# Product-key experts: dense sums for half the tokens, indirect fetches for the other half

## The reference, cut to what matters

```python
q = (h @ w_pq).reshape(B, S, PEER_HEADS, 2, PEER_QHALF)             # 8 heads, 2 halves of 128
s = jnp.einsum('bshjd,hjnd->bshjn', q, sub_keys)                     # 128 keys for each half
v1, i1 = lax.top_k(s[..., 0, :], 16); v2, i2 = lax.top_k(s[..., 1, :], 16)
# 16 x 16 sums of pairs, again the top 16; index of the expert = i1 * 128 + i2
gate = jax.nn.softmax(top_s, axis=-1)
u = jnp.take(expert_u, ib, axis=0)                                   # 128 experts per token
a = jnp.einsum('tkd,td->tk', u, hb)
w = gb * jax.nn.gelu(a, approximate=False)
out = jnp.einsum('tk,tkd->td', w, jnp.take(expert_v, ib, axis=0))    # 16384 experts, rows of 1024 floats
```

## Time and profile before

| | |
|---|---|
| median of 3 runs | 2202.58 us (2202.4 to 2205.08) |
| the profiled execution | 2205.34 us |
| its span, first to last instruction | 2203.6 us |
| TensorE, matmuls | 2012.5 us busy, 91% |
| VectorE | 1316.8 us, 60% |
| ScalarE | 679.1 us, 31% |
| GpSimd | 499.6 us, 23% |
| DMA queue q1 | 276.10 MB, 34.5% of 16 engines |

### The profile page before, as it was taken

The page is one execution under the profiler, slowest core; times in us unless marked ns, Lnnn a source line. Parts: engine busy times, 40 slices in busy tenths (PEclk is TensorE's granted clock), DMA queues, the critical chain, the costliest instruction groups (busy, mean ns, idle before and its releaser), DMA issues.

```text
span 2203.6 us, 25778 instructions
## 1 busy us (share of the span) xinstructions
PE 2012.5 (91%) x9280; PEld 1654.8 (75%) x9280; DVE 1316.8 (60%) x2260; ACT 679.1 (31%) x1074; POOL 499.6 (23%) x305
## 2 busy tenths in 40 slices
PE   5998876969987777899999999999999999999997
PEld 4777555747775777788788888888888888888886
DVE  6545677349997899655445544554555455445544
ACT  4113342342322788412222212222221222122212
POOL 1877424027776677100000000000000000000000
PEclk7899678979998999999999999999999999999999
DMA  8243000422232666754322422342233224322430
GB/s 320 105 191 153 1 0 3 150 95 71 78 115 86 210 206 196 251 187 151 131 95 95 172 113 95 114 171 95 95 137 149 95 95 152 133 95 95 168 118 38
DMA packets 124158, 276.65 MB, mean 126 GB/s; under 512 B 4816, under 2 KB 70352, under 8 KB 116560
## 3 DMA queue, kind: packets, MB, share of 16 engines
q1 hardware_dynamic: 124112, 276.10, 34.5%
HBM read 233.10 MB, written 42.99 MB: 125 GB/s over the span
## 4 chain that ended last, share of the span: by engine, by line
PE 58%; DVE 0%; ACT 0%; DVEq 0%; issue 0%; ACTq 0%
PE bank L1815 27%; PE bank L1841 26%; PE bank L1830 6%; DVE u_raw L1802 0%; DVE rows L1788 0%; ACT L1727 0%; DVE u L1736 0%; DVEq L1588 0%; ACT u L1680 0%; ACT v_raw L1723 0%; DVE rows L1768 0%; DVE rows L1779 0%; ACT act_out L1705 0%; ACTq L1588 0%; DVE rstd L1798 0%
## 5 line engine op out<-in xcount | busy, mean ns | idle before, releaser
L1815 PE MATMUL bank<-actT,u 128*128 128x512 f32 x2592 | 593.7, 390 | 6.9 <-DVE u L1736 4.2
L1841 PE MATMUL bank<-v_parts,w 128*128 128x512 f32 x2496 | 570.0, 389 | 0.0
L1815 PEld LDWEIGHTS bank<-actT,u 128*128 128x128 f32 x2592 | 487.6, 188 | 108.7 <-DVE u L1736 4.3
L1841 PEld LDWEIGHTS bank<-v_parts,w 128*128 128x128 f32 x2496 | 468.6, 188 | 97.1
L1768 DVE TENSOR_TENSOR rows<-rows,bank 128x512 f32<-128x512 f32 x208 | 142.4, 687 | 256.8 <-PE bank L1841 256.8
L1687 ACT ACTIVATE v_parts<-v_raw 128x1024 fp32r<-128x1024 f32 x104 | 109.7, 1055 | 450.9 <-DVE rows L1768 450.4
L1388 PE MATMUL bank<-actT,hl 128*128 128x512 f32 x864 | 212.8, 406 | 31.0 <-POOL hl L1238 27.7
L1747 DVE TENSOR_TENSOR weighed<-act_out,group_gates 128x512 f32<-128x512 f32 x105 | 72.7, 692 | 270.9 <-ACT act_out L1691 270.9
L1388 PEld LDWEIGHTS bank<-actT,hl 128*128 128x128 f32 x864 | 167.6, 197 | 70.1 <-POOL hl L1238 18.2
L1744 DVE TENSOR_TENSOR v_parts<-v_raw,v_parts 128x1024 fp32r<-128x1024 f32 x128 | 156.3, 1221 | 91.9 <-DMA group_gates<-expert_gates 32.3
L1691 ACT ACTIVATE act_out<-bank 128x512 f32<-128x512 f32 x104 | 62.2, 598 | 401.9 <-PE bank L1815 401.9
(11 more groups left out here) (239 smaller groups left out, 2039.3 us busy)
## 6 DMA issues: line engine op xcount, KB each, us to landing
u_raw<-in_u SPq DMA_DIRECT2D x27, 2048.0 KB, 7.4
v_raw<-in_v SPq DMA_DIRECT2D x26, 2048.0 KB, 7.4
expert_gates<-gates SPq DMA_DIRECT2D x16, 2048.0 KB, 8.7
group_gates<-expert_gates SPq DMA_DIRECT2D x32, 1024.0 KB, 6.8
wada<-in_w_ada SPq DMA_DIRECT2D x24, 1024.0 KB, 6.7
v_raw<-in_v SPq DMA_DIRECT2D x24, 512.0 KB, 3.5
raw<-in_u SPq DMA_DIRECT2D x20, 512.0 KB, 3.5
raw<-in_w_cols SPq DMA_DIRECT2D x16, 512.0 KB, 7.3
```

The lines of the kernel that those rows point to most:

```text
L1815: last = nc.tensor.matmul(m.psum[j % banks][:], u[:, p, j, kc * P:(kc + 1) * P], m.actT[:, q, kc, :], start=(kc == 0 and i == 0), stop=(kc ...
L1841: last = nc.tensor.matmul(m.psum[2 + p % 6][:], w[:, x, j, t * P:(t + 1) * P], v[:, z, j, half * S:(half + 1) * S], start=(j == 0 and i == 0),
```

## The change

The tokens are divided. For the first two token tiles (256 tokens, `DT = 2`, `SD = 256`) the dense way stays. For the other two (`LONE = 2`, `SO = 256`) the activations are still computed for all experts, but then only the chosen ones are used: 128 for each token.

- `stage_select`: the early 20 tiles compute the 256 single tokens only (256 columns). It ends with transposes for two token tiles instead of four, and with the list of the single tokens' experts (`own_index`), the address of their activations (`own_at`) and their gates (`own_gate`). The last four loads of u for the next stage are issued here.
- `stage_rest` is new: the other 108 tiles' activations of the single tokens, 256 columns each, gelu, and a store to DRAM. VectorE makes the low part. In ScalarE's order `hi(n)` is followed by the gelu of tile n-2.
- `stage_gates`: 32 rounds instead of 64, with everything else as it was.
- `stage_experts`: all loops are written out. For each of 128 tiles, TensorE does `weighed_sum(n)` (12 matmuls of 512 columns, into four banks that accumulate over the whole stage) and `activate(n + 4)` (24 matmuls of 256 columns, four banks in turn). The high part of the weighed activations goes from VectorE to ScalarE. u and v are loaded tile by tile, the gates group by group into two buffers.
- POOL issues, in the same stage, 256 indirect DMAs that fetch one row of v (4 KB) for each of 128 tokens, into six buffers in turn, and 256 that fetch one activation (4 bytes) for each of 128 tokens. VectorE adds each fetched row, times its weight, to `y` of its token, about 2.17 adds for each of the tiles from number 10 on.
- The squares and gains of all eight results come after the last matmul and the last add.

The diff, cut to its core:

```diff
+DT = TT // 2
+LONE = TT - DT
+SD = DT * P
+SO = LONE * P
+NTB = SD // TB
+FETCH = 6
+CHUNK_K = 16
+LEAD = 4
...
-            def unit(i, u, first):
+            def unit(i, u, first, at=0):
...
-                        last = nc.tensor.matmul(bank[:], hl[:, x, u % m.split, kc * P:(kc + 1) * P],
-                                                m.actT[:, z, kc, :], start=(kc == 0 and j == 0),
+                        last = nc.tensor.matmul(bank[:, 0:S - at], hl[:, x, u % m.split, kc * P:(kc + 1) * P],
+                                                m.actT[:, z, kc, at:], start=(kc == 0 and j == 0),
...
+def stage_rest(nc, a, m):
...
+        count = NKEY - EARLY
...
+        @block.sync
+        def _(sp):
+            def body(i, first):
+                for u in range(RAW):
+                    if not first:
+                        sp.wait_ge(m.unit_lo, i + (n0 - RAW + 1 + u))
+                        sp.dma_start(raw[:, u, :], a.u[bass.ds(i + (EARLY + u), 1), :, :].rearrange("a p f -> p (a f)")
+                                     ).then_inc(m.unit_landed[u], 16)
+                    if not (first and u < 2):
+                        sp.wait_ge(m.unit_evac, i + (e0 + u - 1))
+                        sp.dma_start(m.early[bass.ds(i + (EARLY + u - 2), 1), :, :].rearrange("a p f -> p (a f)"),
+                                     early[:, u % 2, :]).then_inc(rest_stored[u % 2], 16)
...
+        @block.scalar
+        def _(act):
+            def acts(i, k, u, first):
+                act.wait_ge(m.unit_used, i + (n0 + u + 1))
+                if not (first and u < 2):
+                    act.wait_ge(rest_stored[u % 2], k * 32 + 16 * (u // 2))
+                nc.scalar.activation(early[:, u % 2, :], m.psum[u % 2][:, 0:SO], ACT.Gelu).then_inc(m.unit_evac, 1)
+
+            def body(i, k, first):
+                for u in range(RAW):
+                    act.wait_ge(m.unit_landed[u], k * 16 + (n0 // RAW + 1) * 16)
+                    act.wait_ge(m.unit_used, i + (n0 - m.split + 1 + u))
+                    nc.scalar.activation(hl[:, 0, u % m.split, :], raw[:, u, :], ACT.Copy).then_inc(m.unit_hi, 1)
+                    if u >= 2:
+                        acts(i, k, u - 2, first)
+                    elif not first:
+                        acts(i - RAW, k - 1, u + 2, False)
...
-GATE_PAIRS = S // (2 * TB)
+GATE_PAIRS = SD // (2 * TB)
...
+            def fetch_row(n):
+                k, b = divmod(n, LONE)
+                if n >= FETCH:
+                    pool.wait_ge(fetch_read, n - FETCH + 1)
+                nc.gpsimd.indirect_dma_start(
+                    out=fetched[n % FETCH], out_offset=None, in_=rows_of_v,
+                    in_offset=bass.IndirectOffsetOnAxis(ap=m.own_index[:, b, k:k + 1], axis=0)
+                    ).then_inc(fetch_landed[n % FETCH], 16)
...
+            for c in range(chunks):
+                if 1 <= c < chunks - 1:
+                    pool.wait_ge(own_weighed, c)
+                for n in range(each):
+                    if c < chunks - 1:
+                        fetch_act((c + 1) * each + n)
+                    if c * each + n + FETCH < fetches:
+                        fetch_row(c * each + n + FETCH)
...
+            for n in range(-LEAD - 1, tiles):
+                if n + LEAD + 1 < tiles:
+                    hi_of_u(n + LEAD + 1)
+                if 0 <= n + LEAD - 1 < tiles:
+                    gelu(n + LEAD - 1)
+                if 0 <= n + 1 < tiles:
+                    hi_of_w(n + 1)
+                if 0 <= n + 2 < tiles:
+                    hi_of_v(n + 2)
...
+            def add_row(n):
+                k, b = divmod(n, LONE)
+                total = y[:, DT + b, :]
+                dve.wait_ge(fetch_landed[n % FETCH], 16 * (n // FETCH + 1))
...
+                    ins = V.scalar_tensor_tensor(total, fetched[n % FETCH], w3[:, b, k:k + 1], total, ALU.mult, ALU.add)
+                ins.then_inc(fetch_read, 1)
...
+            for n in range(-LEAD - 1, tiles):
+                if 0 <= n + 1 < tiles:
+                    weigh(n + 1)
+                if n + LEAD + 1 < tiles:
+                    lo_of_u(n + LEAD + 1)
+                if 0 <= n + 1 < tiles:
+                    lo_of_w(n + 1)
+                if 0 <= n + 2 < tiles:
+                    lo_of_v(n + 2)
+                own_rows(n)
...
+            for n in range(LEAD):
+                activate(n)
+            for n in range(tiles):
+                weighed_sum(n)
+                if n + LEAD < tiles:
+                    activate(n + LEAD)
```

More of the change, by code:

```diff
@@ L38 @@
 TB = 32
-NTB = S // TB
+DT = TT // 2
[3 more added lines that the diff above has]
+NTB = SD // TB
+SLOTS = PH * TOPK
+FETCH = 6
+CHUNK_K = 16
+LEAD = 4
+ORDER = [(t, half) for t in range(DT, TT) for half in range(2)] + [(t, half) for half in range(2) for t in range(DT)]
 class Steps:
@@ L343, in transpose_pe, with split_act @@
         last.then_inc(transposed, 1)
-def split_act(nc, act, m, actT, banks, piece, transposed, bank_free, piece_lo, hi_ready, modulated, sh, between=None):
+        if after and dc >= 2:
+            after(dc - 2)
+def split_act(nc, act, m, actT, banks, piece, transposed, bank_free, piece_lo, hi_ready, modulated, sh, between=None,
+              turned=None):
     for dc in range(KC):
@@ new lines, in _ @@
+            for n in range(-LEAD - 1, tiles):
[7 more added lines that the diff above has]
+                    hi_of_v(n + 2)
+            act.wait_ge(fetch_read, fetches)
+            for n, (t, half) in enumerate(ORDER):
+                if t < DT:
+                    act.wait_ge(v_used, tiles)
+                x = bank(t, half)[:] if t < DT else y[:, t, half * S:(half + 1) * S]
+                A(square[:, n % 2, :], x, ACT.Square, accum_out=parts[:, half, t:t + 1]).then_inc(squares, 1)
+                act.wait_ge(squares, n + 1)
@@ new lines, in own_rows @@
+            def own_rows(n):
+                slots, steps = fetches, tiles - first_row
+                i = n - first_row
+                if i >= 0:
+                    for r in range(i * slots // steps, (i + 1) * slots // steps):
+                        if r % (LONE * CHUNK_K) == 0:
+                            weigh_own(r // (LONE * CHUNK_K))
+                        add_row(r)
+            for n in range(-LEAD - 1, tiles):
[8 more added lines that the diff above has]
+                own_rows(n)
@@ L1796, in _ @@
+            dve.wait_ge(fetch_read, fetches)
+            for n, (t, half) in enumerate(ORDER):
+                dve.wait_ge(squares, n + 1)
+                part = y[:, t, half * S:(half + 1) * S]
+                x = bank(t, half)[:] if t < DT else part
+                V.tensor_tensor(part, x, m.rowg[:, 1, half * S:(half + 1) * S], ALU.mult).then_inc(gained, 1)
             V.tensor_tensor(m.ss[:], parts[:, 0], parts[:, 1], ALU.add).then_inc(parts_added, 1)
@@ L1820, in early_units, with activate @@
-            def early_units(g, first, final):
-                for j in range(JG):
-                    pe.wait_ge(v_lo, g * JG + (j + 1))
-                    pe.wait_ge(w_ready, g * JG + (j + 1))
-                    if first and j == 0:
-                        pe.wait_ge(gelus, JG)
-                    for p in range(pieces):
-                        t, half = p % TT, p // TT
+            def activate(n):
+                j = n % JG
+                pe.wait_ge(u_lo, n + 1)
+                if n >= JG:
+                    pe.wait_ge(gelus, n - JG + 1)
+                for kc in range(KC):
+                    for i, (p, q) in enumerate(PASSES):
+                        last = nc.tensor.matmul(acts_bank(n)[:, 0:SD], u[:, p, j, kc * P:(kc + 1) * P],
+                                                m.actT[:, q, kc, 0:SD], start=(kc == 0 and i == 0),
+                                                stop=(kc == KC - 1 and i == 2))
+                last.then_inc(a_done, 1)
@@ L1829, in early_units, with weighed_sum @@
+            def weighed_sum(n):
+                j = n % JG
+                pe.wait_ge(v_lo, n + 1)
+                pe.wait_ge(w_ready, n + 1)
+                for half in range(2):
+                    for t in range(DT):
                         for i, (x, z) in enumerate(PASSES):
-                            last = nc.tensor.matmul(m.psum[p][:], w[:, x, j, t * P:(t + 1) * P],
+                            last = nc.tensor.matmul(bank(t, half)[:], w[:, x, j, t * P:(t + 1) * P],
                                                     v[:, z, j, half * S:(half + 1) * S],
-                                                    start=(first and j == 0 and i == 0),
-                                                    stop=(final and j == JG - 1 and i == 2))
@@ L1857, in _ @@
[L1857 to L1865 removed]
+                                                    start=(n == 0 and i == 0), stop=(n == tiles - 1 and i == 2))
+                last.then_inc(v_used, 1)
```

511 lines of the change are left out of this document (250 added, 261 removed).

## The result

The changed kernel takes 2412.31 us (median; 2402.52 to 2418.47 in four runs) against 2203.83 us for the one before in the same session: a ratio of 1.0929, 95% interval 1.0897 to 1.0961. The forecast was 2235 us. The sign was right and the time lies in the range of 2145 to 2480 us, but the loss is 208 us where 32 were forecast.

What follows compares the result with a forecast made beforehand. The prediction took TensorE to bound the old kernel's last stage and DMA transfers the new dense stage: 726 + 605 + 87 + 818 = 2236, plus 1.7 outside the span, less 2.8 to the median, 2235 us; range 2145 to 2480.

Steps and rivals of the forecast that it cites:

- Selection, rest stage, gates: The three stages before the dense stage, forecast at 726, 605 and 87 us.
- The turn of one DMA latency a tile: Rest stage: a queue loop of load, split, gelu and store yields one tile per turn, 5.65 us.
- TensorE's dense tile: Dense stage: TensorE's matmuls take 2.88 + 12 x 0.2267 = 5.60 us a tile, 717 us for 128 tiles.
- rival (5): 256-column matmuls cost the full 188 ns weight load: dense tile 7.2 us, kernel 2361 us; chance 0.04.
- The DMA engines are the bound, 6.2 us a tile: Dense stage: 741 us of transfers plus 55 for activations, 796 us, set the pace.
- 379 GB/s at full share: Dense stage: DMA rate inferred from busy shares in the old trace, making 281 MB take 741 us.
- The 55 us for the activations: Dense stage: 32,768 single activations as 4-byte packets, about 27 ns a packet and engine.
- The cover of POOL's issues: Dense stage: POOL's 512 indirect DMA issues at 1.2 us each take 614 us, hidden.
- bound of 1.55: Dense stage: time per POOL issue, 796/512 = 1.55 us, from which POOL's issuing would decide.
- Rival (3): VectorE stretched beside POOL in the dense stage, 688 us becoming 1022: kernel 2467 us; chance 0.06.
- rival (2): POOL's issue costs more than 1.55 us: kernel 2338 us at 1.75, 2466 at 2.0, 2747 at 2.55; chance 0.21.
- Rival (1): Transfers faster or 4-byte packets free, so TensorE's 717 us paces the dense stage: kernel 2157 us; chance 0.25.

Runs made afterwards that it cites:

- rest_order: Changed kernel with SP, in the rest stage, issuing each load ahead of the store and storing one tile later: 2088 us.
- no_acts: Changed kernel without the 256 fetches of single activations (VectorE weighs constants); the 256 row fetches stay: 2200 us.
- rest_even: rest_order with POOL's issues laid out evenly: first 32 activation fetches over seven tiles, then 4.07 issues in each tile: 1963 us.
- no_rows: Changed kernel without the 256 row fetches (VectorE's row adds run on constants); the 256 activation fetches stay: 2393 us.
- no_fetch: Changed kernel with no indirect DMA at all: POOL's program replaced by two memsets, VectorE's row adds kept: 2194 us.
- no_rows_paced: no_rows with the same activation fetches spread evenly, 2.17 a tile, instead of 32 back to back: 2192 us.
- even_alone: Changed kernel with rest_even's even rhythm of POOL's issues, but the rest stage left as it was: 2371 us.
- roll_pe: Changed kernel with TensorE's dense program as a loop over groups of four tiles, same matmuls, order and waits: 2352 us.
- no_rows_512: no_rows with each of the 256 activation fetches bringing 512 bytes to each partition in place of 4: 2391 us.
- paced: Changed kernel with its activation fetches spread evenly over the tiles, all 512 issues kept, 4.34 a tile: 2378 us.
- rest_even_lead: rest_even with each chunk's activations fetched eight issues further ahead, 40 instead of 32: 2060 us.
- half_desc: Changed kernel with all 512 issues kept, each fetching for 64 partitions instead of 128: 2431 us.
- rest_even_tail: rest_even with the issues spread over 128 tiles instead of 118, 3.75 issues a tile: 1987 us.

## Why the prediction missed

**Selection, rest stage, gates: right.** The turn of one DMA latency a tile was forecast at 5.65 us and is 5.85; the stage at 605 and is 626. The loop load, split, GELU, store, load is confirmed by rest_order, which cuts it at one place and brings the turn to 2.99. Gates 87 and 89.

**TensorE's dense tile: right.** 5.60 us forecast, 5.62 in the stretch without holes; rival (5) is out.

**"The DMA engines are the bound, 6.2 us a tile": the failed step, in the term 741 + 55 = 796.** The 379 GB/s at full share came from a mean over mixed stretches. no_acts moves 409 GB/s with TensorE never pausing, and rest_even 386 with the 4-byte packets among them. The engines carry the stage in TensorE's time; they do not pace it. They may not be far from doing so, as their share is 1.00 to 1.03 in these stretches. The 55 us for the activations were mis-sized as well: there are 8192 packets, not 32,768, and they take 0.3% of no_rows' span, 7 us. The Trainium skill's figure of about 358 GB/s for a core (DMA: Bandwidth & Descriptors, Specifications) was given as speaking against the change. The Trainium skill gets it there by dividing a stack's bandwidth by two cores, and here one core runs; the measurement is above it and decides.

**The cover of POOL's issues: the second half of the same miss, and where the time went.** An issue was taken at 1.2 us. It is 1.25 from start to start at the least (0.95 and 0.30 of idle) and 1.43 in the mean; the bound of 1.55 was not reached. But that bound came from the 796 us of transfers. Against TensorE's 719 us, 512 issues of 1.43 are 732: "614 us, hidden" fails narrowly even by its own reckoning. What costs more is that the step asked only whether POOL has time for its work. It did not ask what the issues do to the engines beside it. That is the loss of 218 us against no_fetch. In the kernel with activation fetches alone it is shown to come from their rhythm: no_rows to no_rows_paced gives back all 201 us. In the full kernel it is shown to need the activation fetches (no_acts), and the same stage ran without the holes in rest_even. None of the rivals had it. Rival (3) was the nearest in kind, but VectorE's subtractions kept their 1.22 us; rival (2) gave a slow POOL, not slow neighbours.

That 2412 lay in the range is luck: it is owed to rival (2)'s width, not to its mechanism. Rival (1), 2157 with TensorE pacing the stage, is close to what the kernel does without the holes: no_fetch 2194, no_acts 2200. Its mechanism was right for the transfers.

Three sums of the prediction are a little off by its own terms, and change nothing above: the transfers that it lists add up to 285 MB and 752 us, not 281 and 741; rival (3) gives 2464, not 2467; rival (5) gives 2370, not 2361.

**What stays open.** Why issues of POOL make TensorE's matmuls come in handfuls and ScalarE's GELU start 11 us late and more (42 in no_rows), and what decides whether they do: neither the number of issues in a run nor their distance tells rest_even from even_alone. It is not the refilling of TensorE's code (roll_pe), nor bytes, the width of a fetch or the table read. A program of ScalarE as a loop was not tried. The Trainium skill (DMA: Bandwidth & Descriptors, SWDGE vs HWDGE vs iDMA) says that a core of POOL computes each descriptor and appends it to rings kept in SBUF. No run here shows whether that path is the one shared.

## What to carry to other kernels

An engine whose queue is "hidden" can still stop its neighbours. When POOL issues indirect DMAs, look in the trace for matmuls that come in handfuls without a wait, and for an engine that waits for a group of matmuls that has long ended. What helped reliably here was to have no more than 2.17 issues in a tile of 5.6 us, with the pauses between them (no_acts, no_rows_paced). At 4.07 a tile the same layout gave a stage of 826 us in one kernel and 932 in another; that rest_even fell on the good side was luck. So a single-core kernel near such an edge should be timed in several layouts. And where a load stands behind a store in one queue, count the loop that goes through it: moving the store back one tile was worth 295 us here.

## What the runs showed of the hardware

- Beside 32 indirect DMAs issued back to back, TensorE fell from 104 matmuls in 16 us to 15 in 20 us, from the 13th to 15th issue on with 4 bytes to a partition and from the 14th to 16th with 512 (no_rows, no_rows_512). The same 256 fetches at 0.39 issues a us cost nothing (2192 us). But 60 issues back to back, 1.42 us apart, stood beside a TensorE without a hole (rest_even).
- In the kernels with the loss ScalarE began some GELUs long after their matmuls had ended (up to 17 us in the kernel after, 42 in no_rows), with 226 to 294 us of waits in all for the kernel after, roll_pe, paced, even_alone, rest_even_lead and half_desc. In no_fetch, no_acts, rest_even and rest_even_tail the trace has no such wait.
- After a hole the granted clock was 0.50, and twelve matmuls of 512 columns took 5.46 us in place of 2.91.
- The 16 DMA engines moved 409 GB/s for 100 us, half of it rows of 4 KB from an indirect DMA, with all engines at work (no_acts).
- An indirect DMA with 128 indices took POOL 0.94 us at the least, 1.13 in the mean and 1.5 when each stood behind a wait; for activations the mean was 1.06 us with 128 indices and 1.08 with 64.
- A matmul of 256 columns with its own weight load came every 120 ns, 24 of them in 2.87 us.
